# Hybrid decoder step: memory projections moved into the recurrent layer and a LayerNorm, recurrent blocks interleaved, weight splits in quarter pieces, high parts written in a row

## Chip, cores and metric

One core of a Trainium2 chip runs the whole step as one program. The metric is the device time of one execution in microseconds (us); lower is better. Engines: PE is TensorE, PEld its weight load, DVE is VectorE, ACT is ScalarE, POOL is GpSimd, SP only issues DMAs. Each has its own queue and waits only on semaphores.

## The reference, cut to what matters

Two layers are computed for 512 prompt tokens and 8 x 4 sample tokens (544 columns), with 1024 features. Layer 0 mixes with a gated linear recurrence (RG-LRU), layer 1 with a gated delta rule over 8 heads. Each then attends to 256 memory tokens and ends in a SwiGLU, dense in layer 0, top 2 of 8 experts in layer 1. Each of the six sub-layers ends in a LayerNorm.

```python
mem_k_p = einsum('bmd,lde->lbme', mem_prompt, xa_wk)      # memory projections, both layers
mem_v_p = einsum('bmd,lde->lbme', mem_prompt, xa_wv)
# recurrent mixer, layer 0
gate_branch, rec = split(x @ w_in)
rec, conv_new = causal_conv(rec, conv0, conv_w, conv_b)
gates = einsum('btnc,ncg->btng', blocks(rec), gate_w) + gate_b
r, i = sigmoid(gates[..., :BW]), sigmoid(gates[..., BW:])
log_a = -8.0 * r * softplus(-lam);  a = exp(log_a)
bterm = sqrt(-expm1(2.0 * log_a)) * i * rec
h[t] = a[t] * h[t-1] + bterm[t]
y = (h * gelu(gate_branch)) @ w_out
# each sub-layer
x = layer_norm(alpha * x + sublayer(x))
```

## The kernel before, in words

Activations stand with features on partitions: x is 8 tiles of 128 x 544. Products that must be close to fp32 are made of three passes in fp32r: an activation is split into a high part (xh, hh) and a low part (xl, hl), a weight tile into wh and wl. One weight tile of 128 outputs is a *slot*: SP loads it into one of four raw buffers, POOL makes wh and wl (`split`, two instructions of 1024 columns, two buffers each), and PE runs 48 matmuls on it in `lin_steps`: wh with xh, wl with xh, wh with xl. A *direct* slot is not split; PE reads raw in full fp32. The memory projections (16 slots a layer, `kv`) are direct. Slots are numbered in the order in which PE uses them, and the semaphores w_in, w_split and w_used count them, so SP, POOL, PE and the engine that evicts all follow one order that is written out by hand. DVE and ACT run their instructions strictly one after the other (`Serial`).

The order on PE: for each of four blocks of the recurrent layer two "rec" tiles, two "gelu" tiles and four gate groups; the output linear of 8 tiles (S_LOUT); LayerNorm 0 with the 16 projections of layer 0; attention 0; LayerNorm 1; the dense FFN (72 slots, PE lines 501 and 674); LayerNorm 2; the 32 matmuls for beta and decay ("wba", L724) and a chain on 8 partitions; 8 heads of the delta rule, where each head's projections of the next head fill PE's gaps; the output linear; LayerNorm 3 with the projections of layer 1; attention 1; LayerNorm 4 with the router; the experts on direct slots.

In a recurrent block ACT copies the rec tiles out, DVE convolves them (lines 1548 to 1558), PE multiplies by the gate weights (L706), which ACT loads at the start of the block into one buffer, ACT applies the sigmoids (L1146), exp, tanh and a square root, and DVE forms the recurrence in a scan. The root's argument 1 - a*a is made from tanh with a reciprocal (L1603). The two tiles of a block go through this one after the other.

A LayerNorm sums on PE (L523), subtracts the mean on DVE (L1433), squares on ACT (L1026), sums squares on PE (L530), multiplies on DVE (L1436), and then ACT writes for each k the high part xh (L1036) and the tile of x (L1038); DVE takes the low part xl (L1422). The next linear's first tile waits for ln_xh tile by tile in its first pass and for ln_xl in its third. In LayerNorms 0 and 3 three projections follow the sum on PE and 13 follow the squares (KV_EARLY = 3), and ACT evicts them between its own instructions.

## Time and profile before

| what | value |
|---|---|
| median of 3 runs | 2915.51 us (2908.92 to 2920.08) |
| profiled execution: time, span | 2916.7 us, 2914.5 us |
| granted TensorE clock, mean | 0.891 of full |
| PE busy | 2439.2 us, 84% of the span |
| DVE, ACT, POOL busy | 961.7, 580.2, 790.2 us |
| chain that ended last, by engine | PE 70%, DVE 16%, ACT 5%, DMA 4% |

The span is cut below by stages, as seen in the timeline: recurrent layer up to 269 us, its output linear to 320, LayerNorm 0 with projections to 388, attention 0 to 549, LayerNorm 1 to 582, dense FFN to 1024, LayerNorm 2 to 1065, beta stage to 1110, heads to 1840, output linear to 1891, LayerNorm 3 with projections to 1959, attention 1 to 2120, LayerNorm 4 and routing to 2200, experts to the end. The granted clock of PE is 1.00 at 2.4 GHz and 0.5 at 1.2 GHz; a value between is a mean over the stretch.

### The profile page before, as it was taken

The numbers are of one execution on the slowest core, as the hardware profiler recorded it, in microseconds if no ns is written. First come the engines' busy times: TensorE is split into PE (matmuls) and PEld (weight loads), VectorE is DVE, ScalarE is ACT, GpSimd is POOL, SyncE is SP. The second block draws the span as 40 slices with busy tenths as digits, with TensorE's granted clock in tenths as the row PEclk, the third lists the DMA queues.
The fourth block names the chain that finished last, engine by engine and source line by source line (L and its number), as shares of the span: only waits on it lengthen the run. The fifth ranks groups of instructions, "written<-read, shape, count | busy, mean of one in ns | idle before, by whom it ended". The sixth has DMA issues, their size and how long they took to land.

```text
span 2914.5 us, 42825 instructions
## 1 busy us (share of the span) xinstructions
PE 2439.2 (84%) x17284; PEld 2293.5 (79%) x17284; DVE 961.7 (33%) x1473; ACT 580.2 (20%) x1086; POOL 790.2 (27%) x389
## 2 busy tenths in 40 slices
PE   6664998899999945888777886899959999999994
PEld 5654895799999925887767875897748999999994
DVE  6774302411011046565556564321240100000003
ACT  2232312211001032322233222032130000000113
POOL 4421250477677602221111220314310000000001
PEclk9876999899999976887777886899969999999996
DMA  5112444122222201111111110354125667777885
GB/s 196 51 43 74 149 141 159 58 80 86 81 86 87 86 15 46 46 47 45 40 44 45 45 46 16 106 195 170 59 91 188 207 193 240 248 250 263 281 279 169
DMA packets 97656, 346.06 MB, mean 119 GB/s; under 512 B 13440, under 2 KB 18688, under 8 KB 92528
## 3 DMA queue, kind: packets, MB, share of 16 engines
q1 hardware_dynamic: 73136, 279.08, 29.6%
q10 hardware_dynamic: 18368, 43.60, 4.3%
q0 software_dynamic: 6016, 21.43, 2.1%
q8 instruction: 101, 1.65, 0.2%
q14 instruction: 35, 0.29, 0.0%
HBM read 317.61 MB, written 26.47 MB: 118 GB/s over the span
## 4 chain that ended last, share of the span: by engine, by line
PE 70%; DVE 16%; ACT 5%; DMA 4%; issue 2%; POOL 0%; DVEq 0%; ACTq 0%; SPq 0%; POOLq 0%
PE ps L501 25%; PE ps L951 13%; PE ps L966 7%; PE ps L674 5%; DVE work L1551 2%; DMA raw<-weights 2%; PE ps L552 2%; PE ps L548 2%; PE ps L530 2%; PE ps L797 2%; PE ps L706 1%; PE ps L809 1%; DVE work L1553 1%; PE ps L806 1%; PE ps L781 1%
## 5 line engine op out<-in xcount | busy, mean ns | idle before, releaser
L426 POOL TENSOR_TENSOR wh<-raw,tab 128x1024 fp32r<-128x1024 f32 x168 | 323.7, 1927 | 1343.3 <-PE ps L501 1150.6
L951 PE MATMUL ps<-work,raw 128*128 128x128 f32 (+6 forms) x3072 | 423.8, 299 | 15.7 <-DMA raw<-weights 12.4
L428 POOL TENSOR_TENSOR wl<-raw,wh 128x1024 fp32r<-128x1024 f32 x168 | 430.7, 2564 | 13.2
L951 PEld LDWEIGHTS ps<-work,raw 128*128 128x128 f32 x3072 | 419.3, 191 | 18.9 <-issue 6.9
L501 PE MATMUL ps<-xh,wh 128*128 128x272 f32 x2048 | 310.5, 304 | 71.4 <-ACT work L1126 28.7
L501 PEld LDWEIGHTS ps<-xh,wh 128*128 128x128 f32 x2048 | 284.0, 200 | 78.2 <-issue 41.4
L501 PE MATMUL ps<-xh,wl 128*128 128x272 f32 x2048 | 289.2, 291 | 0.0
L501 PE MATMUL ps<-xl,wh 128*128 128x272 f32 x2048 | 285.7, 289 | 0.0
L501 PEld LDWEIGHTS ps<-xh,wl 128*128 128x128 f32 x2048 | 270.2, 191 | 0.3
L501 PEld LDWEIGHTS ps<-xl,wh 128*128 128x128 f32 x2048 | 265.9, 188 | 0.0
L966 PE MATMUL ps<-work,raw 128*128 128x128 f32 (+6 forms) x1536 | 217.9, 298 | 1.1 <-DVE work L1878 0.8
L966 PEld LDWEIGHTS ps<-work,raw 128*128 128x128 f32 x1536 | 209.6, 190 | 1.9 <-DVE work L1878 1.4
L470 POOL DMA_DIRECT2D rows_y<-moe_h x8 | 4.3, 538 | 658.6 <-DVE moe_h L1871 658.6
L1878 DVE TENSOR_TENSOR work<-moe_h,ps 128x128 f32<-128x128 f32 (+6 forms) x96 | 30.7, 319 | 441.3 <-ACT moe_h L1354 441.3
L1354 ACT ACTIVATE moe_h<-ps 128x128 f32<-128x128 f32 (+6 forms) x96 | 29.1, 303 | 399.1 <-PE ps L951 399.0
L1500 DVE TENSOR_TENSOR work<-work,ps 128x544 f32<-128x544 f32 x24 | 17.3, 722 | 232.0 <-PE ps L501 232.0
L1551 DVE SCALAR_TENSOR_TENSOR work<-work 128x568 f32<-128x568 f32 x64 | 90.0, 1407 | 2.3
L1871 DVE COPY moe_h<-ps 128x256 f32<-128x256 f32 (+1 forms) x64 | 25.1, 392 | 197.6 <-PE ps L939 155.7
L674 PE MATMUL ps<-hh,wh 128*128 128x272 f32 x384 | 80.8, 292 | 5.9 <-DVE hl L1422 5.9
L674 PE MATMUL ps<-hh,wl 128*128 128x272 f32 x384 | 79.9, 291 | 0.0
L674 PE MATMUL ps<-hl,wh 128*128 128x272 f32 x384 | 79.9, 290 | 0.0
L706 PE MATMUL ps<-work 128*128 128x272 f32 x128 | 41.1, 491 | 38.5 <-DMA work<-lru_gate 33.8
...
## 6 DMA issues: line engine op xcount, KB each, us to landing
raw<-weights SPq DMA_DIRECT2D x488, 512.0 KB, 3.8
...
moe_h<-rows_x POOLq DMA_DIRECT2D x14, 512.0 KB, 8.0
rows_x<-lnsq ACTq DMA_DIRECT2D x9, 512.0 KB, 7.1
...
```

Source lines behind the costliest of these rows:

```text
L426: nc.gpsimd.tensor_tensor(flat(h1), flat(r1), one_col, MUL).then_inc(pool_hi, 1)
L428: nc.gpsimd.tensor_tensor(flat(l1), flat(r1), flat(h1).bitcast(F), SUB).then_inc(w_split, 1)
L501: last = mm(ps[:, 2 * i + h, 0:HT], w[:, par_, k, :], a[:, k, h * HT:(h + 1) * HT], start=(n == 0 and k == 0), stop=(n == 2 and k == KT - 1))
L530: last = mm(ps[:, 6 + h, 0:HT], ones, lnsq[:, k % 2, h * HT:(h + 1) * HT], start=(k == 0), stop=(k == KT - 1))
L548: last = mm(ps[:, b, 0:MEM], raw[:, q, k, :], A_mem[:, k, :], start=(k == 0), stop=(k == KT - 1))
L552: last = mm(ps[:, b, mt * P:(mt + 1) * P], A_mem[:, k, mt * P:(mt + 1) * P], raw[:, q, k, :], start=(k == 0), stop=(k == KT - 1))
L674: last = mm(ps[:, 2 * d + h, 0:HT], w[:, s % 2, k, :], a[:, f, h * HT:(h + 1) * HT], start=(f == 0 and m == 0), stop=(f == FT - 1 and m == 2))
L706: last = mm(ps[:, 4 + 2 * (g % 2) + h, 0:HT], L_gw[:, 4 * k + g, :], L_rec[:, k, h * HT:(h + 1) * HT], start=(k == 0), stop=(k == 1))
L797: last = mm(ps[:, 4, c * P:(c + 1) * P], G_bl[:, v % 2, c, :], G_t[:, c, :], start=True, stop=True)
L951: last = mm(ps[:, j // 2, (j % 2) * c:(j % 2 + 1) * c], raw[:, slot % RAW, k, :], M_x[:, r % 2, k, 0:c], start=(k == 0), stop=(k == KT - 1))
L966: last = mm(ps[:, 2 + d % 2, 0:c], raw[:, slot % RAW, k, :], M_h[:, f, 0:c], start=(f == 0), stop=(f == FT - 1))
L1551: s(V.scalar_tensor_tensor(acc, ext[:, j:j + CONV], w(j), acc, MUL, ADD))
```

## The change

- **Projections of layer 0.** They leave LayerNorm 0 and go into the recurrent layer: four before the first rec tiles, four after the first gelu tiles, four after the second, four after the last gates. Memory, its first weights and x are loaded in another order at the start. Keys and values get room that the recurrent layer leaves free.
- **Projections of layer 1.** They leave LayerNorm 3: seven go into LayerNorm 2, nine behind the wba matmuls. ACT evicts the nine between the steps of the beta chain.
- **Recurrent layer.** PE runs block b+1's rec tiles ahead of block b's gates. DVE convolves block b+1 ahead of block b's recurrence. Buffers are doubled, the gate weights of block b+1 are loaded after block b's sigmoids, loops are unrolled, and the root's argument is (1 + a*a) * tanh, without a reciprocal.
- **wba.** The two groups of 8 outputs go to partitions 0 and 32 of the same banks, and each k waits for its own tile of x.
- **Splits.** POOL makes each high and each low part in four instructions of 256 columns (PIECES = 4).
- **LayerNorm.** ACT writes the eight high parts in a row, then the eight tiles of x.

The core of the diff; most removed lines and repeated parts are left out:

```diff
-KV_EARLY = 3
+KV_EARLY, KV_MID = 3, 7
...
-RAW, SPLIT = 4, 2
+RAW, SPLIT, PIECES = 4, 2, 4
...
+        S_KV0 = [0, 8, 16, 28]
+        S_LRU = [4, 12, 20, 24]
+        S_LOUT = 32
+        S_Q = [S_LOUT + 8, None]
         S_O = [S_Q[0] + 8, None]
         S_FFN = S_O[0] + 8
...
+        S_KV1 = S_FFN + HALVES * 36
+        S_GDN = S_KV1 + 16
...
+        A_v = moe_h[:, S0:S0 + MT * D].rearrange("p (a b) -> p a b", b=D)
+        A_k = moe_h[:, S1:S1 + KT * MEM].rearrange("p (a b) -> p a b", b=MEM)
...
+            load(0, None, W_KV0, 0, 2)
+            sp.dma_start(x[:, :, :], I["xT"]).then_inc(ld_x, 16)
+            load(0, None, W_KV0, 2, 4)
+            turns(S_LRU[0], RAW, None, None, W_LRU)
+            turns(S_KV0[1], RAW, 4, None, W_KV0 + 4)
+            turns(S_LRU[1], RAW, None, None, W_LRU + 4)
+            turns(S_KV0[2], RAW, 8, None, W_KV0 + 8)
+            turns(S_LRU[2], RAW, None, None, W_LRU + 8)
+            turns(S_LRU[3], RAW, 12, None, W_LRU + 12)
+            turns(S_KV0[3], RAW, 12, None, W_KV0 + 12)
+            turns(S_LOUT, 8, None, 16, W_LOUT)
             for l in range(NL):
...
+                d = 16 * (l + 1)
+                turns(S_Q[l], 8, d, d, W_Q0 if l == 0 else W_Q1)
+                turns(S_O[l], RAW, d, d, (W_Q0 if l == 0 else W_Q1) + 8)
+                cache(l)
+                turns(S_O[l] + RAW, RAW, d, d, (W_Q0 if l == 0 else W_Q1) + 8 + RAW)
                 if l == 0:
...
+                    turns(S_FFN, HALVES * 36, 16, 16, W_FFN)
+                    turns(S_KV1, 16, 16, None, W_KV1)
+                    turns(S_GDN, 4 * GH + 8, None, 32, W_GDN)
...
-                    nc.gpsimd.tensor_tensor(flat(h1), flat(r1), one_col, MUL).then_inc(pool_hi, 1)
-                    pool.wait_ge(pool_hi, t * RAW + (j + 1 - offset))
-                    nc.gpsimd.tensor_tensor(flat(l1), flat(r1), flat(h1).bitcast(F), SUB).then_inc(w_split, 1)
+                    for q in range(PIECES):
+                        k0, k1 = q * KT // PIECES, (q + 1) * KT // PIECES
+                        nc.gpsimd.tensor_tensor(flat(h1[:, k0:k1]), flat(r1[:, k0:k1]), one_col, MUL).then_inc(pool_hi, 1)
+                    for q in range(PIECES):
+                        k0, k1 = q * KT // PIECES, (q + 1) * KT // PIECES
+                        pool.wait_ge(pool_hi, PIECES * t * RAW + (PIECES * (j - offset) + q + 1))
+                        low = nc.gpsimd.tensor_tensor(flat(l1[:, k0:k1]), flat(r1[:, k0:k1]), flat(h1[:, k0:k1]).bitcast(F), SUB)
+                    low.then_inc(w_split, 1)
...
                 if l is not None:
-                    kv(l, KV_EARLY, 16)
+                    kv(l, KV_EARLY, KV_MID)
...
+                    if l == 0 and 4 <= t < 12 and t % 4 < 2:
+                        pe.wait_ge(lru_gelu, 2 * (t // 4) - 2 + t % 4 + 1)
+                    elif l == 0 and t >= 12 and t % 4 < 2:
+                        pe.wait_ge(lru_gelu, 6 + t % 4 + 1)
+                    elif t >= 2:
+                        pe.wait_ge(kv_ev, 16 * l + t - 1)
...
+            def lru_rec(b):
                 for j in range(2):
...
+                    if b in (1, 2, 0):
+                        pe.wait_ge(kv_ev, 4 * b + 3 + j)
+                    else:
+                        pe.wait_ge(lru_gelu, 2 * (b - 1) + j + 1)
+                    lin_tile(S_LRU[b] + j, 4 * (min(b, 2) + 1), j, j, xh, xl, fresh=0 if b == 0 and j == 0 else None,
...
+            def lru_gel(b):
                 for j in range(2):
...
+                    pe.wait_ge(lru_ext, 2 * b + j + 1)
+                    lin_tile(S_LRU[b] + 2 + j, 4 * (min(b, 2) + 1), j, j, xh, xl)
+            def lru_gates(b):
+                pe.wait_ge(lru_gw_in, 16 * (b + 1))
+                pe.wait_ge(lru_conv, 2 * b + 2)
                 for g in range(4):
...
+                    ge(pe, lru_gate_ev, 4 * b + g - 1)
                     for k in range(2):
                         for h in range(2):
                             last = mm(ps[:, 4 + 2 * (g % 2) + h, 0:HT], L_gw[:, 4 * k + g, :],
...
+                                      L_rec[:, b % 2, k, h * HT:(h + 1) * HT], start=(k == 0), stop=(k == 1))
                     last.then_inc(lru_gate_full, 1)
...
+            kv(0, 0, 4)
+            lru_rec(0)
+            lru_gel(0)
+            kv(0, 4, 8)
+            lru_rec(1)
+            lru_gates(0)
+            lru_gel(1)
+            kv(0, 8, 12)
+            lru_rec(2)
+            lru_gates(1)
+            lru_gel(2)
+            lru_rec(3)
+            lru_gates(2)
+            lru_gel(3)
+            lru_gates(3)
+            kv(0, 12, 16)
+            pe.wait_ge(kv_ev, 16)
             pe.wait_ge(lru_y, 8)
...
-            layer_norm(0, 0)
+            linear(S_LOUT, 16, hh, hl, z_ready, 0)
...
-            layer_norm(2)
-            pe.wait_ge(ln_xl, KT * 3)
-            for g in range(2):
...
-                        last = mm(ps[0:GH, 4 + 2 * g + h, 0:HT], pc("wba", 16 * k + 8 * g, 16 * k + 8 * g + 8),
+            layer_norm(2, 1)
+            for k in range(KT):
+                pe.wait_ge(ln_x, KT * 2 + k + 1)
+                for h in range(2):
+                    for g in range(2):
+                        last = mm(ps[32 * g:32 * g + GH, 4 + h, 0:HT], pc("wba", 16 * k + 8 * g, 16 * k + 8 * g + 8),
                                   x[:, k, h * HT:(h + 1) * HT], start=(k == 0), stop=(k == KT - 1))
             last.then_inc(b_pe, 1)
+            kv(1, KV_MID, 16)
+            pe.wait_ge(kv_ev, 32)
...
+            act.dma_start(A_mem, I["memT"].rearrange("p (a b) -> p a b", b=MEM)).then_inc(mem_in, 16)
             act.dma_start(tab[:, :], I["tables"]).then_inc(ld_tab, 16)
...
+            kv(0, 0)
+            kv(0, 1)
             act.wait_ge(ld_x, 16)
             for k in range(KT):
                 s(A(xh[:, k, :], x[:, k, :], ACT.Copy), x_split_h, k + 1)
+            kv(0, 2)
+            kv(0, 3)
...
+                if n < NLN - 1:
+                    for k in range(KT):
+                        act.wait_ge(ln_n, n * KT + k + 1)
+                        s(A(xh[:, k, :], x[:, k, :], ACT.Identity, bias=pc("lnb", n * 8 + k, n * 8 + k + 1),
+                            scale=pc("lng", n * 8 + k, n * 8 + k + 1)), ln_xh, n * KT + k + 1)
                 for k in range(KT):
                     act.wait_ge(ln_n, n * KT + k + 1)
-                    if n < NLN - 1:
...
                     s(A(x[:, k, :], x[:, k, :], ACT.Identity, bias=pc("lnb", n * 8 + k, n * 8 + k + 1),
                         scale=pc("lng", n * 8 + k, n * 8 + k + 1)), ln_x, n * KT + k + 1)
...
+                    if l is not None and k < KV_MID - KV_EARLY:
...
+            def sigmoid(b):
+                ge(act, lru_dve, 6 * (b - 1) + 6)
                 for g in range(4):
...
+                    act.wait_ge(lru_gate_full, 4 * b + g + 1)
                     dst = (L_r, L_i)[g // 2]
...
+                    s(A(two(dst[:, g % 2, :]), pair(2 + g % 2), ACT.Sigmoid, bias=lgb[:, 2 * b + g % 2, g // 2:g // 2 + 1]),
+                      lru_gate_ev, 4 * b + g + 1)
+                if b + 1 < BLK:
+                    gate_weights(b + 1)
+            def decays(b):
                 for j in range(2):
...
+                    act.wait_ge(lru_dve, 6 * b + j + 1)
+                    s(A(L_a[:, j, :], L_r[:, j, :], ACT.Exp, scale=-1.0))
+                    s(A(L_t[:, j, :], L_r[:, j, :], ACT.Tanh), lru_act, 4 * b + j + 1)
+            def root(b, j):
+                act.wait_ge(lru_dve, 6 * b + j + 3)
+                s(A(L_t[:, j, :], L_t[:, j, :], ACT.Sqrt), lru_act, 4 * b + j + 3)
+            def high_part(b, j):
+                act.wait_ge(lru_dve, 6 * b + j + 5)
+                s(A(hh[:, 2 * b + j, :], L_b[:, j, :], ACT.Copy), lru_yh, 2 * b + j + 1)
+            ext(0)
+            gelu(0)
+            for t in range(4, 8):
+                kv(0, t)
+            for b in range(BLK - 1):
+                ext(b + 1)
+                sigmoid(b)
+                decays(b)
+                root(b, 0)
+                root(b, 1)
+                gelu(b + 1)
+                high_part(b, 0)
+                high_part(b, 1)
+                if b == 0:
+                    for t in range(8, 12):
+                        kv(0, t)
+            b = BLK - 1
+            sigmoid(b)
+            decays(b)
+            kv(0, 12)
+            root(b, 0)
+            root(b, 1)
+            kv(0, 13)
+            high_part(b, 0)
+            kv(0, 14)
+            high_part(b, 1)
+            kv(0, 15)
+            kv_out(0)
             act.wait_ge(lru_y, 8)
...
-            layer_norm(0, 0)
+            piece(0, 0)
+            act.wait_ge(w_used, S_LOUT + 8)
+            piece(0, 1)
+            piece(0, 2)
...
+            act.wait_ge(w_used, S_KV1)
+            act.dma_start(A_mem, I["memT"].rearrange("p (a b) -> p a b", b=MEM)).then_inc(mem_in, 16)
+            layer_norm(2, 1)
             act.wait_ge(b_pe, 1)
             s(A(two(B_r[1])[0:GH], pair(2)[0:GH], ACT.Sigmoid), b_act, BETA)
+            kv(1, KV_MID)
             act.wait_ge(b_dve, ARGUMENT)
             s(A(B_r[5][0:GH, :], B_r[5][0:GH, :], ACT.Exp, scale=-1.0))
             s(A(B_r[9][0:GH, 0:1], pc("alog")[0:GH, :], ACT.Exp), b_act, RATE)
+            for t in range(KV_MID + 1, 13):
+                kv(1, t)
             act.wait_ge(b_dve, SUMS)
             s(A(B_r[2][0:GH, :], B_r[0][0:GH, :], ACT.Exp))
             s(A(B_r[3][0:GH, :], B_r[3][0:GH, :], ACT.Exp), b_act, GROWN)
+            for t in range(13, 16):
+                kv(1, t)
+            kv_out(1)
             act.wait_ge(b_dve, ROWED)
...
-            kv_start(1)
-            layer_norm(3, 1)
+            act.wait_ge(w_used, S_GOUT + 8)
+            for i in range(RING):
+                piece(1, i)
+            layer_norm(3)
...
-                    s(V.tensor_scalar(L_b, L_t, 1.0, None, ADD))
-                    s(V.reciprocal(L_b, L_b))
-                    s(V.scalar_tensor_tensor(L_t, L_t, 2.0, L_b, MUL, MUL), lru_dve, b * 10 + (3 * j + 5))
...
+                    dve.wait_ge(lru_act, 4 * b + j + 1)
+                    s(V.tensor_tensor(L_b[:, j, :], L_a[:, j, :], L_a[:, j, :], MUL))
+                    s(V.scalar_tensor_tensor(L_t[:, j, :], L_b[:, j, :], 1.0, L_t[:, j, :], ADD, MUL), lru_dve, 6 * b + j + 3)
+                for j in range(2):
+                    k = 2 * b + j
...
+                    dve.wait_ge(lru_act, 4 * b + j + 3)
+                    s(V.tensor_tensor(bt, t, L_i[:, j, :], MUL))
...
+                    s(V.tensor_tensor_scan(t, a, bt, 0.0, MUL, ADD))
...
+                    dve.wait_ge(lru_gelu, 2 * b + j + 1)
+                    s(V.tensor_tensor(bt, t, L_gel[:, 2 * (b % 2) + j, :], MUL), lru_dve, 6 * b + j + 5)
+                for j in range(2):
+                    k = 2 * b + j
+                    dve.wait_ge(lru_yh, 2 * b + j + 1)
+                    split_low(hl[:, k, :], L_b[:, j, :], hh[:, k, :], lru_y, 2 * b + j + 1)
+            lru_convolve(0)
+            for b in range(BLK):
+                if b + 1 < BLK:
+                    lru_convolve(b + 1)
+                lru(b)
```

## Rows read from the trace of the kernel before

**Rows 1.** Windows: stretch, length, busy PE PEld DVE ACT POOL, clock, DMA share, GB/s.

```profile
0.00:10.00 10.00, 0.00 (x0) 0.00 (x0) 0.00 (x0) 1.28 (x1) 1.15 (x5) 1.00 0.81 310
24.00:269.00 245.00, 146.72 (x897) 135.98 (x897) 165.26 (x224) 76.31 (x105) 75.41 (x32) 0.78 0.18 58
582.00:1024.00 442.00, 434.58 (x3442) 433.75 (x3440) 47.20 (x65) 33.75 (x51) 314.22 (x143) 0.99 0.27 84
1110.00:1840.00 730.00, 579.89 (x3824) 531.87 (x3824) 423.93 (x655) 201.21 (x387) 145.19 (x64) 0.79 0.14 42
```

**Rows 2.** Groups by line, 95 to 270 us: busy, mean ns, idle before.

```profile
L1603 DVE RECIPROCAL work<-work 128x544 f32<-128x544 f32 x7 | 24.9, 3553 | 0.2
```

**Rows 3.** The chain that ended last, whole span: start, us, what.

```profile
0.76 9.48 DMA x<-xT
...
107.06 4.19 DMA work<-lru_gate
...
227.81 10.34 PE ps L706 x32
...
341.10 17.27 PE ps L548 x80
358.37 28.60 PE ps L552 x256
```

**Rows 4.** Timeline around LayerNorms 0 and 1: start, us, engine, line, operation.

```profile
317.42 2.16 PE L501 MATMUL ps<-hl,wh 128*128 128x272 f32 x16
...
391.60 2.16 PE L501 MATMUL ps<-xl,wh 128*128 128x272 f32 x16
...
546.74 1.91 PE L501 MATMUL ps<-xl,wh 128*128 128x272 f32 x14
...
578.86 0.84 ACT L1036 ACTIVATE xh<-x,par 128x544 fp32r<-128x544 f32 x1
...
585.38 2.16 PE L501 MATMUL ps<-xl,wh 128*128 128x272 f32 x16
```

**Rows 5.** Timeline, router in LayerNorm 4.

```profile
2150.78 5.39 PE L900 MATMUL ps<-par,x 128*128 128x8 f32 x40
```

**Rows 6.** Timeline: sample scores, then the beta stage, on PE.

```profile
441.94 1.91 PE L568 MATMUL ps<-moe_h 128*32 128x256 f32 x32
...
1065.02 17.07 PE L724 MATMUL ps<-x,par 128*8 128x272 f32 x64 [17.25 <-DVE xl L1422]
...
1107.24 1.98 PE L731 MATMUL ps<-tab,work 8*128 8x8 f32 x20 [25.14 <-DVE work L1659]
```

**Rows 7.** The page's DMA issues: count, KB, us to landing.

```profile
raw<-weights SPq DMA_DIRECT2D x488, 512.0 KB, 3.8
```

**Rows 8.** Timeline: POOL at start and in the FFN, small DVE.

```profile
0.26 0.10 POOL L2028 MEMSET const-float32-0.0<- 128x1 f32 x1 [0.26 <-issue]
...
0.75 0.95 POOL L415 MEMSET lnsq<- 128x1024 f32 x1 [0.29 <-POOLq L2028]
...
28.16 0.17 DVE L1519 TENSOR_TENSOR work<-work 128x8 f32<-128x8 f32 x1
...
623.62 1.89 POOL L426 TENSOR_TENSOR wh<-raw,tab 128x1024 fp32r<-128x1024 f32 x1 [1.16 <-PE ps L501]
625.59 2.39 POOL L428 TENSOR_TENSOR wl<-raw,wh 128x1024 fp32r<-128x1024 f32 x1
...
631.65 2.77 POOL L428 TENSOR_TENSOR wl<-raw,wh 128x1024 fp32r<-128x1024 f32 x1
```

**Rows 9.** Timeline, recurrent layer, POOL and DVE.

```profile
161.02 2.34 POOL L428 TENSOR_TENSOR wl<-raw,wh 128x1024 fp32r<-128x1024 f32 x1
161.09 2.85 DVE L1621 TENSOR_TENSOR work<-work 128x544 f32<-128x544 f32 x1
```

**Rows 10.** The chain in one head.

```profile
1465.23 2.75 DVE work L1553
...
1482.22 0.76 DVE work L1553
```

283 lines of the change are left out of this document (106 added, 177 removed).

## The prediction

> **What bounds the kernel now.** I read the stage windows first, then the chain that ended last, then the timeline of each stage the diff touches. PE is the bound on average, but it is full only in some stages: 434.6 of 442 us in the dense FFN, against 146.7 of 245 us in the recurrent layer and 579.9 of 730 us in the gated-delta heads [rows 1]. In the recurrent layer the chain alternates between PE gates, a 3.55 us reciprocal per tile on DVE, and a gate-weight load of 4.2 to 4.5 us before each of blocks 1 to 3 [rows 2, 3]. Nothing is queued on PE for those times. The 16 memory-projection tiles of a layer are the opposite case: they sit in LayerNorms 0 and 3, and their 13 later tiles run as one unbroken PE block on the chain, 17.3 us for five key tiles and 28.6 us for eight value tiles [rows 3]. So there is idle PE in one place and 56 us of movable PE work in another.
>
> The profiled execution took 2916.7 us around a span of 2914.5; the median of the three runs is 2915.5, so I sum against 2916.7 and take 1 us off.
>
> **LayerNorms 0 and 3.** From the end of the linear before to the end of the first tile after, LayerNorm 0 takes from 319.6 to 393.6, 74.0 us. LayerNorm 1, which has no projections, takes from 548.7 to 587.4, 38.7 us, its cold PE included [rows 4]. The projections leave, so 35.3 us leave, twice. LayerNorm 3's window has the same length. The cache pieces that ACT loads keep their conditions and are needed over 80 us later.
>
> **High parts in a row.** ACT needs 0.84 us and a gap of 0.03 for each of the 16 writes [rows 4]. Before, the eighth high part came 14 us after the first write began, and two more passes of 16 matmuls followed. Now it comes after 7 us, the middle pass follows at once, and the last pass is paced by x tiles that still end at 14 us: last x, 0.8 us for its low part, two matmuls. The first tile ends near 583.6 in place of 587.4 in LayerNorm 1's times, so -3.8 us for each of LayerNorms 0, 1 and 3. LayerNorm 4 goes the other way. Its consumer reads x, not the high parts, so it starts 6 us later; 40 router matmuls take 10.8 us there (two groups, one of 5.4 us [rows 5]) plus 2.8 us of transposes. That ends near 2160.3 in place of 2156.2: +4. Sum of these parts with the 35.3 twice: -70.6 - 11.4 + 4 = -78.
>
> **LayerNorm 2 and the beta stage.** Seven projections go into LayerNorm 2, nine behind the 32 wba matmuls. By LayerNorm 0's old pacing, the seven delay the last x tile by about 11 us, to 1074.6. But the wba matmuls now go k by k behind ln_x and no longer wait for all the low parts. Their two groups write column groups 0 and 1. 16 score matmuls of 32 columns, in four column groups, took 1.9 us (32 records), 0.12 us each, against 0.43 for a full-width one of the same 256 columns (17.3 us for 40) [rows 3, 6]: different column groups run together. So wba costs about 7.5 us in place of 17.1, mostly under ln_x, and ends near 1076.5 in place of 1082.1. Nine projections of 3.5 us then end at 1108.6, and kv_ev 32 holds the 8-row transposes to 1109.2; they stood at 1107.2 behind the DVE chain [rows 6], which this change starts 5.6 us earlier and so hides. The first head tile then starts 2 us later, warm, and saves about 2. I take 0, bounds -3 and +8. If wba did not pair up it would be +8.
>
> **Recurrent layer.** Start: x now queues behind two weight tiles, while ACT's queue brings the memory, tables and gates. About 5.9 MB must pass before x is complete, at the 310 to 350 GB/s of the start [rows 1]; x lands near 17.5 us and not at 10.2 [rows 3]. Four projections fill PE meanwhile; splitting x again takes its time, and the first tile starts as if at 27.5 (24.2 before).
> PE's list from there to the last gelu tile: 16 tiles of 6.0 us (a tile's period, from the starts at 625.59 and 631.65 [rows 8]), 8 projections of 3.5 us, 3 gate groups. A gate group took 10.3 us because PE was at half clock in its first part. Kept busy, 16 matmuls of 272 columns cost 16 x 0.43 x 272/256 = 7.3 us. 27.5 + 96 + 28 + 22 = 173.5.
> DVE decides the end. It had 165 us in 245, 41 per block. Each block loses two reciprocals and adds (8.0 us), gains two multiplies (1.5) and drops the parameter copies (some 1): 34 per block, lock waits included. The third block's recent part starts about 156 (end of rec 3), conv 3 and lru 2 end near 181, and sigmoid 3 waits for that, so two gates stand until 181 and end at 185.5. The last block's own tail was 30.7 us, from the gates' end at 238.2 [rows 3] to 268.9. Two reciprocals with their adds go (8.0), one exp and one sqrt table load (2.6), and the two halves overlap on ACT and DVE: 18. Projections 12 to 15, 14.3 us, lie inside that. 185.5 + 18 = 203.5, and I add 5 for splits that DVE's work stretches, see below: 209. That is -60, bounds -40 and -75. Each recurrent tile's 0.5 MB load waits on SP behind a projection's release: 3.8 us to land [rows 7] and 4.4 to split, 8.2 of the 10.5 us that three more projections take, so hidden with 2 us to spare; the projections' evictions (0.38 us each on ACT) and the two output DMAs have ACT's idle time. The gate-weight loads are issued a block ahead, at no cost while three PE groups stand between; without that cover 4.5 each.
>
> **Split in eight pieces.** This touches every split slot. A POOL instruction and a DVE one with two SBUF inputs exclude each other: a 0.73 us multiply that began at 161.09 took 2.85, to just past the end of the POOL piece at 163.36, then its own time [rows 9]. With quarter pieces a single DVE wait is at most a quarter as long, but POOL comes back four times as often. For a lone DVE instruction that is a gain; for a burst that outlasts the split, the total blocked time is POOL's own, before and after. Heads have both kinds: L1553 took 2.75 beside a split and 0.76 without [rows 10]; four such waits per head, 6.8 us, lie on the chain, and two of the three places are bursts. I take 0 for the heads, bounds -40 and +20.
> The price is the fixed cost of six more instructions. A slot has 6.06 us; POOL uses 1.89 + 0.08 + 2.39, or 2.77 where DVE interferes, so 1.7 or 1.3 us are free: 0.22 to 0.28 us per added instruction [rows 8]. No row shows a quarter piece. From below: a one-column memset took 0.10. From above: if multiply moved data as fast as the 1024-column memset (0.95), the fixed part were 1.0 us. The nearest in kind is DVE's TENSOR_TENSOR of 8 columns, 0.17 us; it fits under the limit, so 0 [rows 8]. The added POOL time in the heads, 1 us a split, is inside their bounds.
>
> The Trainium skill ("SBUF — State Buffer", section "SBUF: two separate sides") says that the shared port pair is an exclusive lock held for the whole instruction, which the two durations above bear out. Taken alone it favours short pieces, the third rival below. Its page "GPSIMD Engine Reference", section "Performance versus the Vector engine", gives 4497 ns for a two-input fp32 operation of 2048 columns; with 2.39 for our 1024 that is an estimate of 0.28 us fixed, at the limit, which speaks against this edit and belongs to the first rival.
>
> **Sum.** -78 + 0 - 60 + 0 = -138. 2916.7 - 138 - 1 = 2778.
>
> **Rivals.**
> *POOL becomes the bound of the full stages.* 72 FFN and 48 linear tiles have the 6.06 us period. At 0.30 us fixed the slot is short by 0.1 or 0.5, at 0.4 by 0.7 or 1.1: 36 to 108 us over 120 tiles, 2815 to 2885. For it: the free time is under a third of the slot, and nothing measures a piece. Against: the 0.10 us of the small memset and the 0.17 of DVE. Chance 0.18.
> *The recurrence stays chain-bound.* Serial waits of ACT and DVE, and splits stretched to 8 us while DVE is busy, keep the output linear at 235. 2804. For: DVE was busy 67% and its lock waits are in that. Chance 0.14.
> *Short pieces free DVE.* Of the 6.8 us per head, 5 go, 8 times: 2738. Chance 0.14.
> *Slower.* One mechanism: an added POOL instruction costs over 0.42 us. From there the shortage, 6 x 0.42 - 1.5 = 1.05 us, times 120 plus some 12 for the heads, eats the whole 138; at 0.5 it is 180 + 15, so 2778 + 195 = 2973. The bound of 1.0 from above allows it. Chance 0.07.
> The forecast itself has 0.47, range 2755 to 2803.
>
> **Numbers.** The range reaches from the freed DVE to most of the POOL case: 2735 to 2865. A difference under 0.5% (15 us) can't be told from none. Faster: all but the slow case and the thin edge before it, 0.91; same 0.02; slower 0.07.
>
> **What would show it.** Output linear of the recurrent layer starting near 209, gate groups near 7.3 us, no gate-weight wait on the chain; 35 us between the linears around LayerNorms 0 and 3; no projection in either; quarter POOL pieces under 0.65 us (high) and 0.8 (low), POOL idle at each FFN slot and PE's FFN still near 442; wba near 8 us. Wrong if PE waits for POOL in the FFN, if PE idles before gate groups, or if the heads' 88 us period moves by over 3 us.

## The result and the profile after

The changed kernel takes 2772.0 us (median of 4 runs, 2767.2 to 2775.8) against 2915.2 for the kernel before on the same chip, a ratio of 0.951 (0.9485 to 0.9534). The forecast was 2778. That the sum came this close is partly luck: gains of 20.9 us that it had missed and losses of 17.9 us that it had missed nearly cancel (last point of the account below). Milestones read from PE's timeline, in us of the two profiled executions (spans 2914.5 and 2773.5):

| stretch | before | after | change | predicted |
|---|---|---|---|---|
| start to output linear of the recurrent layer | 268.9 | 213.3 | -55.6 | -60 |
| LayerNorm 0, to the end of the next first tile | 74.0 | 32.9 | -41.1 | -39.1 |
| LayerNorm 1, same | 38.7 | 32.2 | -6.6 | -3.8 |
| dense FFN | 436.4 | 437.4 | +1.0 | 0 |
| LayerNorm 2 and beta, to the first head tile | 86.1 | 90.3 | +4.2 | 0 |
| heads, to their output linear | 731.2 | 717.6 | -13.6 | 0 |
| LayerNorm 3, as 0 | 73.7 | 32.2 | -41.6 | -39.1 |
| LayerNorm 4, to the experts' first transposes | 70.8 | 79.1 | +8.3 | +4 |
| linears, attentions, experts | | | +4.0 | 0 |
| sum | | | -141.0 | -138 |

The window of the recurrent layer of the kernel after, up to the last gelu tile (columns as in [rows 1]):

```profile
28.00:182.00 154.00, 149.52 (x1058) 142.51 (x1059) 96.76 (x162) 55.29 (x88) 91.12 (x120) 0.99 0.39 129
```

PE is busy 149.5 of 154 us, where it had 146.7 of 245 in the whole layer before [rows 1], at a granted clock of 0.99. Its own timeline, with the idle time ahead of a row and its releaser in brackets:

```profile
27.86 3.77 PE L534 MATMUL ps<-xh,wh 128*128 128x272 f32 x16 [2.23 <-issue]
...
129.91 3.95 PE L748 MATMUL ps<-work 128*128 128x272 f32 x16 [0.33 <-ACT work L1210]
...
147.67 2.24 PE L534 MATMUL ps<-xh,wh 128*128 128x272 f32 x16 [1.81 <-POOL wl L458]
...
155.63 2.24 PE L534 MATMUL ps<-xh,wh 128*128 128x272 f32 x16 [1.72 <-POOL wl L458]
...
187.43 5.63 PE L748 MATMUL ps<-work 128*128 128x272 f32 x16 [1.91 <-ACT work L1210]
192.89 14.45 PE L589 MATMUL ps<-raw,work 128*128 128x128 f32 x128
213.32 1.93 PE L534 MATMUL ps<-hh,wh 128*128 128x272 f32 x7 [5.97 <-DVE hl L1528]
```

The gate-weight loads are gone from PE's waits. Two new waits are for POOL; its timeline there shows why. A split in quarters takes about 5.2 us where DVE does not interfere (5.16 in the FFN, shown below). Beside DVE's recurrence four low pieces take 4.26 us and the four high pieces behind them 3.79, together more than the 6 us of a tile:

```profile
143.26 4.26 POOL L458 TENSOR_TENSOR wl<-raw,wh 128x256 fp32r<-128x256 f32 x4
147.49 3.79 POOL L454 TENSOR_TENSOR wh<-raw,tab 128x256 fp32r<-128x256 f32 x4
151.24 4.24 POOL L458 TENSOR_TENSOR wl<-raw,wh 128x256 fp32r<-128x256 f32 x4
```

The router in LayerNorm 4 before, PE's timeline (its second group is [rows 5]), and the window of both groups (PE, PEld, DVE, ACT, POOL, clock, DMA, GB/s):

```profile
2140.38 1.26 PE L900 MATMUL ps<-par,x 128*128 128x8 f32 x10 [4.19 <-ACT x L1038]
2142.13 6.11 PE L900 MATMUL ps<-par,x 128*128 128x8 f32 x30 [0.48 <-ACT x L1038]
...
2140.30:2156.30 16.00, 15.31 (x92) 14.80 (x92) 9.22 (x14) 13.59 (x18) 0.00 (x0) 0.64 0.00 1
```

The beta stage and the router after, and the window of the router. The router's first group starts behind 10.30 us of idle time in place of 4.19. Its second group of 40 takes 7.96 us in place of 5.39, at a granted clock of 0.50 in the whole window in place of 0.64. The wba group takes 7.51 us in place of 17.1 [rows 6] and waits for nothing. What waits in LayerNorm 2 are the projections ahead of it, 3.81 us, for an eviction (L1080) that stands on ACT behind the eight high parts:

```profile
961.24 9.84 PE L585 MATMUL ps<-work,raw 128*128 128x256 f32 x32 [3.81 <-ACT moe_h L1080]
971.01 7.51 PE L782 MATMUL ps<-x,par 128*8 128x272 f32 x64
...
1995.72 8.12 PE L960 MATMUL ps<-par,x 128*128 128x8 f32 x40 [10.30 <-ACT x L1120]
...
2006.39 7.96 PE L960 MATMUL ps<-par,x 128*128 128x8 f32 x40
...
1995.70:2014.40 18.70, 18.63 (x92) 18.17 (x92) 5.80 (x8) 7.67 (x10) 0.00 (x0) 0.50 0.00 1
```

The chain of waits of the kernel after has something new at the start of the heads: a store of the rows of beta, which go through DRAM. In the kernel before, this store is not among DVE's waits there. Now 2 MB of keys and values are issued on ACT's queue right ahead of it:

```profile
1013.67 9.96 DMA scratch<-work
...
1024.54 4.67 DMA work<-gdn_hist
```

### The profile page after: what moved, and what is told of

Read it like the earlier page. It is cut to its first block, busy times and chain, and to the rows that moved or that the text cites. A ratio compares the mean times of both kernels' runs of the same rounds, so it can differ in the third digit from the quotient of the medians.

```text
span 2773.5 us, 43947 instructions
## 1 busy us (share of the span) xinstructions
PE 2434.3 (88%) x17284; PEld 2290.4 (83%) x17284; DVE 868.2 (31%) x1445; ACT 569.5 (21%) x1078; POOL 980.2 (35%) x1397
## 4 chain that ended last, share of the span: by engine, by line
PE 75%; DVE 10%; ACT 6%; DMA 5%; issue 2%; POOL 1%; ACTq 0%; DVEq 0%; SPq 0%; POOLq 0%
PE ps L534 29%; PE ps L1011 13%; PE ps L1026 8%; PE ps L710 5%; DMA raw<-weights 3%; PE ps L563 2%; PE ps L857 2%; PE ps L585 2%; PE ps L869 2%; PE ps L589 2%; PE ps L866 1%; PE ps L841 1%; PE ps L921 1%; DVE x L1542 1%; PE ps L623 1%
## 5 line engine op out<-in xcount | busy, mean ns | idle before, releaser
L454 POOL TENSOR_TENSOR wh<-raw,tab 128x256 fp32r<-128x256 f32 x672 | 433.7, 676 | 1016.3 <-PE ps L534 816.4
L458 POOL TENSOR_TENSOR wl<-raw,wh 128x256 fp32r<-128x256 f32 x672 | 517.8, 800 | 0.0
L1011 PEld LDWEIGHTS ps<-work,raw 128*128 128x128 f32 x3072 | 419.6, 191 | 20.9 <-issue 13.7
L534 PE MATMUL ps<-xh,wh 128*128 128x272 f32 x2048 | 316.1, 306 | 24.9 <-ACT xh L1116 11.1
L534 PEld LDWEIGHTS ps<-xh,wh 128*128 128x128 f32 x2048 | 284.1, 200 | 36.7 <-issue 26.1
L585 PE MATMUL ps<-work,raw 128*128 128x256 f32 x256 | 61.9, 405 | 13.2 <-DMA work<-memT 7.1
L1559 DVE SCALAR_TENSOR_TENSOR x<-x,ps 128x544 f32<-128x544 f32 x32 | 23.1, 721 | 157.8 <-PE ps L534 157.8
```

Of the source, the lines that this page charges most:

```text
L454: nc.gpsimd.tensor_tensor(flat(h1[:, k0:k1]), flat(r1[:, k0:k1]), one_col, MUL).then_inc(pool_hi, 1)
L458: low = nc.gpsimd.tensor_tensor(flat(l1[:, k0:k1]), flat(r1[:, k0:k1]), flat(h1[:, k0:k1]).bitcast(F), SUB)
L534: last = mm(ps[:, 2 * i + h, 0:HT], w[:, par_, k, :], a[:, k, h * HT:(h + 1) * HT], start=(n == 0 and k == 0), stop=(n == 2 and k == KT - 1))
L585: last = mm(ps[:, b, 0:MEM], raw[:, q, k, :], A_mem[:, k, :], start=(k == 0), stop=(k == KT - 1))
L1011: last = mm(ps[:, j // 2, (j % 2) * c:(j % 2 + 1) * c], raw[:, slot % RAW, k, :], M_x[:, r % 2, k, 0:c], start=(k == 0), stop=(k == KT - 1))
```

## The experiments

A ratio is the kernel's time over that of the kernel before, both measured on the same chip; between experiments, ratios are compared. The changed kernel itself has 0.951. Milestones come from one profiled execution of each kernel.

### Pieces: whole splits in the changed kernel

```diff
-RAW, SPLIT, PIECES = 4, 2, 4
+RAW, SPLIT, PIECES = 4, 2, 1
```

> The changed kernel with each split in two whole instructions again. My theory after reading the trace of the changed kernel: the short pieces, priced at 0 in the prediction, gave most of the 2.6 us per head and part of the 6.4 us of LayerNorm 1. Then the heads' period goes from 85.3 back to about 88 us, LayerNorm 1 from 32.3 to about 34.5, the dense FFN from 437.3 to about 436, and the time from 2772 to about 2797. Rival: the heads and the LayerNorms are shorter because PE's clock is granted higher (0.906 against 0.891) since the projections went; then whole splits change the heads by under 0.5 us each and the time stays within 5 us of 2772. Second rival: the 8 us by which the last gelu tile comes late are the price of the pieces (PE waited for POOL twice); then the recurrent layer's output linear starts near 205 in place of 213.

Measured: 2797.9 us, ratio 0.9599 (0.9569 to 0.9629). Heads 734.1 us in place of 717.6, their period (from one head's first tile to the next head's) up to 87.9 in place of 85.3; LayerNorms 0 and 3 both 34.0 in place of 32.9 and 32.2, LayerNorm 1 32.7, FFN 435.1, output linear at 215.5. PE's clock is 0.904 here too, so the clock's rival falls, and so does the one that put the late gelu tile down to the pieces (it ends at 181.0). The first theory holds for the heads; in LayerNorm 1 the pieces gave 0.5 us, not 2.

What the pieces do in a head is seen in the same burst of DVE in both kernels. With whole splits, the timeline of DVE and POOL:

```profile
1207.46 1.89 POOL L454 TENSOR_TENSOR wh<-raw,tab 128x1024 fp32r<-128x1024 f32 x1 [9.45 <-PE ps L534]
1207.95 4.82 DVE L1656 SCALAR_TENSOR_TENSOR work<-work 128x568 f32<-128x568 f32 x2
1209.43 2.73 POOL L458 TENSOR_TENSOR wl<-raw,wh 128x1024 fp32r<-128x1024 f32 x1
1212.81 0.75 DVE L1658 SCALAR_TENSOR_TENSOR work<-work 128x512 f32<-128x512 f32 x1
1213.59 0.25 DVE L1662 SCALAR_TENSOR_TENSOR work<-work 128x28 f32<-128x28 f32 x1
1213.87 0.22 DVE L1663 SCALAR_TENSOR_TENSOR work<-work 128x4 f32<-128x4 f32 x1
```

With quarter pieces, the kernel after:

```profile
1203.04 3.87 POOL L454 TENSOR_TENSOR wh<-raw,tab 128x256 fp32r<-128x256 f32 x4 [7.63 <-PE ps L534]
1203.53 1.89 DVE L1656 SCALAR_TENSOR_TENSOR work<-work 128x568 f32<-128x568 f32 x2
1205.45 0.98 DVE L1658 SCALAR_TENSOR_TENSOR work<-work 128x512 f32<-128x512 f32 x1
1206.47 0.48 DVE L1662 SCALAR_TENSOR_TENSOR work<-work 128x28 f32<-128x28 f32 x1
1206.87 3.75 POOL L458 TENSOR_TENSOR wl<-raw,wh 128x256 fp32r<-128x256 f32 x4
1206.98 0.62 DVE L1663 SCALAR_TENSOR_TENSOR work<-work 128x4 f32<-128x4 f32 x1
```

In this burst the two engines take turns. With whole splits two DVE instructions pay for the split's 4.6 us, and the burst of five takes 6.1 us. With quarters each DVE instruction waits for one piece, even the small ones (0.48 and 0.62 us for 0.25 and 0.22), the burst takes 4.1, and it is POOL that is late: 7.6 us for the split. POOL is not among PE's nine largest waits in the heads; DVE heads that list, with 35.7, 35.3 and 24.0 us. Over all heads DVE's busy time, which includes its waits for POOL, falls from 422.4 to 396.4 us, and POOL's rises from 144.9 to 205.9. Two groups of DVE's lines over all heads, whole and then quarters:

```profile
L1656 DVE SCALAR_TENSOR_TENSOR work<-work 128x568 f32<-128x568 f32 x48 | 71.0, 1479 | 1.7
L1829 DVE TENSOR_TENSOR work<-work,tab 128x512 f32<-128x512 f32 x56 | 60.1, 1073 | 1.9
```

```profile
L1656 DVE SCALAR_TENSOR_TENSOR work<-work 128x568 f32<-128x568 f32 x48 | 46.6, 971 | 1.7
L1829 DVE TENSOR_TENSOR work<-work,tab 128x512 f32<-128x512 f32 x56 | 43.1, 770 | 1.9
```

### Pieces alone in the kernel before

```diff
-RAW, SPLIT = 4, 2
+RAW, SPLIT, PIECES = 4, 2, 4
...
-                    nc.gpsimd.tensor_tensor(flat(h1), flat(r1), one_col, MUL).then_inc(pool_hi, 1)
+                    for q in range(PIECES):
...
+                        nc.gpsimd.tensor_tensor(flat(h1[:, k0:k1]), flat(r1[:, k0:k1]), one_col, MUL).then_inc(pool_hi, 1)
...
```

> The kernel before with nothing but the splits in quarter pieces. If the pieces free DVE at short waits and cost PE nothing: heads' period 88 to about 85.5, LayerNorms 1, 2 and 4 some 2 us shorter each, dense FFN 436 to 437.5, recurrent layer within 3 us of 269; time about 2915 - 27 = 2888. If the heads' gain comes from elsewhere: within 5 us of 2915. If the pieces cost where PE is full, over 2920.

Measured: 2880.6 us, ratio 0.9869 (0.9843 to 0.9896). Heads 713.8 us in place of 731.2, FFN 439.3, LayerNorms 1, 2 and 4 at 37.8, 84.7 and 71.5. The heads came as expected, the LayerNorms hardly moved, and what I had not expected is the recurrent layer: its output linear starts at 245.6 in place of 268.9. There DVE's busy time falls from 165.3 to 148.7 us and PE's waits for ACT's copies (L1126) from 28.7 to 12.7 us. That DVE's waits lay on that layer's chain in the kernel before fits both, but no run separates them. In the changed kernel the same pieces are worth 2.2 us.

### Output transfers behind the rows

```diff
-            kv_out(1)
             act.wait_ge(b_dve, ROWED)
...
             rows(0)
+            kv_out(1)
```

> The changed kernel with the two output transfers of layer 1's keys and values (2 MB) issued behind the rows of the first head and not ahead of the scratch store. Theory: they held the scratch store up for 8 us, which the first head's convolution waited for, and that is why the heads gained 13.6 us and not 21. Then the store lands about 2 us after its issue, the output linear of the gated-delta layer starts 7 to 9 us earlier against the first head tile, and the time is 2772 - 8 = 2764. Rival: the first head has slack, since PE has other tiles; then the store is early and the time stays at 2772 within 3 us.

Measured: 2774.6 us, ratio 0.9504 (0.9474 to 0.9533): no difference. DVE's wait for the scratch store falls from 10.6 to 3.4 us, but its wait for ACT behind the convolution grows from 6.1 to 10.0. From the first head tile to the second head's first tile it is 54.7 us in place of 56.4, so at most 1.7 us of the 8 counted. Even these are not sure: with the reciprocal put back (below) and the transfers left where they were, that stretch is 54.8 us too. The chain between them, in this kernel, runs through the splits of the next tiles:

```profile
1019.93 2.33 POOL wh L454 x4
1022.26 3.62 POOL wl L458 x4
```

The theory was wrong in size: the wait was real and mostly covered. (The heads' stretch was 713.6 here, but 2.9 of those 4 us come in the last head, whose end is 147.7 or 150.6 us from one run to the next, with either place of the transfers.)

### Order of ACT's writes, tile by tile

```diff
-                if n < NLN - 1:
-                    for k in range(KT):
-                        act.wait_ge(ln_n, n * KT + k + 1)
-                        s(A(xh[:, k, :], ...), ln_xh, n * KT + k + 1)
                 for k in range(KT):
                     act.wait_ge(ln_n, n * KT + k + 1)
+                    if n < NLN - 1:
+                        s(A(xh[:, k, :], ...), ln_xh, n * KT + k + 1)
                     s(A(x[:, k, :], ...), ln_x, n * KT + k + 1)
```

> The changed kernel with ACT writing high part and tile of x in turn for each k, as before. The prediction priced the row order at -3.8 us for each of LayerNorms 0, 1 and 3 and +4 for LayerNorm 4. By that: LayerNorms 0 and 3 from 33.0 and 32.2 to about 36.5, LayerNorm 1 from 32.3 to 36, LayerNorm 4's stretch to the first transposes from 79.1 to 75; the time goes up by about 7 us to 2779. By what the trace of after shows (+8.2 in LayerNorm 4) the sum is only +3: 2775. Rival: the order is worth nothing because DVE's low parts pace the third pass either way; then LayerNorm 1 stays within 1 us.

Measured: 2778.4 us, ratio 0.951 (0.948 to 0.954). LayerNorms 0, 1 and 3: 37.8, 37.0 and 36.7 us, so the row order is worth 4.9, 4.8 and 4.5. LayerNorm 4: 71.8 in place of 79.1, so it costs 7.3 there. LayerNorm 2 with beta: 85.7 in place of 90.3, a cost of 4.6 that I had not priced at all. Net 14.2 - 11.9, some 2 us, which the two times can't tell apart. In LayerNorm 4 the router starts 7.1 us sooner than in the changed kernel, at the same clock (0.50). In LayerNorm 2 it is not wba that gains: the last four of the seven projections take 13.9 us without a wait in place of 20.7 with the wait for the eviction, and wba now waits 0.8 us for tiles of x.

### The reciprocal put back

```diff
-                    s(V.tensor_tensor(L_b[:, j, :], L_a[:, j, :], L_a[:, j, :], MUL))
-                    s(V.scalar_tensor_tensor(L_t[:, j, :], L_b[:, j, :], 1.0, L_t[:, j, :], ADD, MUL), ...)
+                    s(V.tensor_scalar(L_b[:, j, :], L_t[:, j, :], 1.0, None, ADD))
+                    s(V.reciprocal(L_b[:, j, :], L_b[:, j, :]))
+                    s(V.scalar_tensor_tensor(L_t[:, j, :], L_t[:, j, :], 2.0, L_b[:, j, :], MUL, MUL), ...)
```

> The changed kernel with the root's argument made from tanh with an add and a reciprocal again, as in the kernel before (one DVE instruction more per tile, the reciprocal among them). Theory: PE bounds the recurrent layer up to the last gelu tile (it is busy 149.5 of the 154 us from 28 to 182), so DVE's extra time is hidden in the first three blocks and counts in the last block's tail alone: 2 x (3.6 + 0.7 - 1.0) = about 6.5 us. Then the last gelu tile ends at 182 as now, and the output linear starts at 213 + 6.5 = 220; time 2772 + 6 = 2778. Rival: DVE's chain paces every block; then all four blocks lose 6.5 us and the linear starts at 239, the time is 2798.

Measured: 2799.5 us, ratio 0.9602 (0.9586 to 0.9618); last gelu tile at 191.8, last gates at 210.8, output linear at 236.5. My theory fell: 23 us, near the rival's 26. Some 10 us are lost up to the last gelu tile and 13 behind it. PE's waits in this layer, in the kernel with the reciprocal (total, times, longest):

```profile
PE ps L748 <- ACT work L1210: 9.3, 4, 8.3
PE ps L534 <- ACT work L1203: 5.2, 1, 5.2
...
PE ps L589 <- ACT work L1203: 4.3, 1, 4.3
```

L1203 is the gelu. It stands on ACT behind the roots, and a root waits for DVE's argument, as ACT's timeline of block 0 shows:

```profile
96.58 1.28 ACT L1223 ACT_TABLE_LOAD   x1 [3.59 <-DVE work L1694]
...
101.42 0.66 ACT L1223 ACTIVATE work<-work 128x544 f32<-128x544 f32 x1 [2.89 <-DVE work L1694]
102.09 1.28 ACT L1203 ACT_TABLE_LOAD   x1
```

Without the reciprocal the gelu's table load starts at 95.8 and its second tile waits for PE instead. So a busy PE (149.5 of 154) did not mean slack on DVE: the two were level, through ACT's queue.

### No filler between the recurrent blocks

Loads, splits and evictions follow the new numbers, and x is loaded first.

```diff
-        S_KV0 = [0, 8, 16, 28]
-        S_LRU = [4, 12, 20, 24]
+        S_KV0 = [16, 20, 24, 28]
+        S_LRU = [0, 4, 8, 12]
...
-            kv(0, 12, 16)
+            kv(0, 0, 16)
```

> The changed kernel with all 16 projections of layer 0 behind the last gates; the rest of the recurrent layer as it is. Theory: PE's list sets the pace, so without its 8 middle projections (27.8 us) and with x loaded first the last gelu tile ends some 30 us earlier, near 150, and the gates near 163; of the 56 us of projections some 20 lie under the last block's tail and the linear starts near 163 + 57 = 220, 7 us later than now: only about half of the filler is free. Rival: the recurrence's own chain of ACT and DVE sets the pace and the fillers are all free; then the last gates still end near 190 and the linear starts near 247, and the time is 2772 + 34 = 2806.

Measured: 2784.2 us, ratio 0.955 (0.9534 to 0.9566); last gelu tile ends at 153.4, last gates at 164.6, output linear starts at 221.4. As expected of PE's list. Moving 12 projections, 42 us of PE work, into the blocks and the start saves 8 us over leaving them all at the end. What the new order of the blocks gives by itself, without the shorter argument and the pieces, was not run.

### x first, and mixed order

Both have the output transfers behind the rows. In the one, LayerNorms 2 and 4 write the tiles of x first and then each high part as a copy of its tile; in the other they write tile by tile. LayerNorms 0, 1 and 3 keep the row order.

```diff
-                if n < NLN - 1:
+                if n in (0, 1, 3):
...
+                if n in (2, 4):
+                    for k in range(KT):
+                        s(A(xh[:, k, :], x[:, k, :], ACT.Copy), ln_xh, n * KT + k + 1)
```

> The changed kernel with the output transfers of keys and values behind the first head's rows, and in LayerNorms 2 and 4, where PE's next work reads x, the eight tiles of x ahead of the eight high parts (each then a copy of its tile). With tile by tile in every LayerNorm the two stretches took 85.7 and 71.8 us in place of 90.3 and 79.1; here the last tile of x comes 7 us earlier still. Theory: LayerNorm 2 with beta about 82 us, LayerNorm 4 to the first transposes about 68, heads 714: 2772 - 8 - 11 - 4 = 2749. Rival: DVE's chains behind the low parts, which now come last, eat it; then 86 and 76, about 2762.

Measured: 2758.5 us, ratio 0.9465 (0.9449 to 0.9481); LayerNorm 2 with beta 83.5, LayerNorm 4 72.7, heads 717.5.

> As the kernel with x first, but LayerNorms 2 and 4 write tile by tile as the kernel before, LayerNorms 0, 1 and 3 keep the high parts in a row. By the run with tile by tile everywhere: LayerNorms 0, 1, 3 at 33, 32, 32 us, LayerNorm 2 with beta 85.7, LayerNorm 4 71.8, heads 714: 2772 - 4.6 - 7.3 - 4 = 2756. If the order's price in LayerNorm 4 was the clock and not the order, LayerNorm 4 stays near 79 and the time is 2763.

Measured: 2758.8 us, ratio 0.946 (0.9444 to 0.9476); LayerNorm 2 with beta 85.7, LayerNorm 4 70.9, heads 717.3. Both beat the changed kernel by about 13 us. In LayerNorm 4 x first brings nothing more, as PE's timeline of that kernel shows:

```profile
1979.68 8.12 PE L960 MATMUL ps<-par,x 128*128 128x8 f32 x40 [3.32 <-ACT x L1120]
...
1990.36 7.96 PE L960 MATMUL ps<-par,x 128*128 128x8 f32 x40
```

and the mixed order's:

```profile
1986.45 1.22 PE L960 MATMUL ps<-par,x 128*128 128x8 f32 x10 [4.19 <-ACT x L1123]
1988.20 6.11 PE L960 MATMUL ps<-par,x 128*128 128x8 f32 x30 [0.53 <-ACT x L1123]
...
1996.86 5.38 PE L960 MATMUL ps<-par,x 128*128 128x8 f32 x40
```

PE waits 3.3 us in place of 4.2: tile by tile it was not starved for long anyway (0.53 us). And with x first the router's matmuls ran at a granted clock of 0.50 (1979.6 to 1998.4) in place of 0.64 (1986.4 to 2002.3), so that the second group took 7.96 us and not 5.38. That is more than the 1.8 us by which x first is behind, so the order by itself gained a little there and the clock took it back.

### Halves and eighths

```diff
-RAW, SPLIT, PIECES = 4, 2, 4
+RAW, SPLIT, PIECES = 4, 2, 2
```

and the same with 8, both on the mixed-order kernel.

> The mixed-order kernel with splits in four pieces, halves, in place of eight quarters. A whole instruction (1.9 to 2.4 us) gave a heads' period of 87.9 us, a quarter 85.3. If DVE's wait goes with the length of the piece, halves give half of what separates them from none: the period would be 85.3 + (87.9 - 85.3) x (1/2 - 1/4)/(1 - 1/4) = 86.2, the heads 723 in place of 717.3, the time 2759 + 6 = 2765; the dense FFN 0.5 to 1 us shorter. Rival: a DVE burst needs one gap only, so halves do all: period 85.3, time 2757. Second rival: only quarters help, since a half is still longer than the DVE instructions: 87.9, time 2775.

Measured: 2764.2 us, ratio 0.9485 (0.9466 to 0.9503); period 86.2 to 87.7, heads 724.2, FFN 437.9. As expected: between whole splits and quarters, what the heads lose goes with the length of the piece.

> The mixed-order kernel with splits in sixteen pieces of 128 columns. Uncontended, a split took 2.33 + 2.82 = about 5.1 us in quarters against 4.36 whole: 0.13 us for each added instruction. Eight more make 6.2 us, over PE's 6.0 us a tile: POOL becomes the bound in the dense FFN and the linears, 0.2 to 0.5 us a tile. Expected: dense FFN from 438 to 452 to 475 us, each linear of 8 tiles 2 to 4 us longer, the heads no better than 717; time 2759 + 25 to 60, about 2800. Rival: the fixed cost shrinks with the piece and POOL stays under the slot: 2757.

Measured: 2833.8 us, ratio 0.9719 (0.9698 to 0.974); FFN 475.3, attentions 163 and 162 in place of 156, LayerNorms 0 and 3 39.0, heads 714.2 in place of 717.3. The FFN came at the end of my range and the time above it, since I had left out the attentions and LayerNorms. The heads were even a little shorter than the 717 that I had set as their best. Tiles of the FFN start at 605.54, 611.76 and 618.47 here, 6.2 and 6.7 us apart. The splits without DVE beside them, from POOL's timeline in the FFN, whole (kernel before, at 599.62), halves, quarters and eighths, one fence for each of the last three:

```profile
498.51 2.04 POOL L454 TENSOR_TENSOR wh<-raw,tab 128x512 fp32r<-128x512 f32 x2 [0.98 <-PE ps L534]
500.51 2.53 POOL L458 TENSOR_TENSOR wl<-raw,wh 128x512 fp32r<-128x512 f32 x2
```

```profile
497.75 2.33 POOL L454 TENSOR_TENSOR wh<-raw,tab 128x256 fp32r<-128x256 f32 x4 [0.41 <-PE ps L534]
500.03 2.83 POOL L458 TENSOR_TENSOR wl<-raw,wh 128x256 fp32r<-128x256 f32 x4
```

```profile
527.89 2.91 POOL L454 TENSOR_TENSOR wh<-raw,tab 128x128 fp32r<-128x128 f32 x8
530.76 3.39 POOL L458 TENSOR_TENSOR wl<-raw,wh 128x128 fp32r<-128x128 f32 x8
```

1.89 + 2.39 = 4.28 us in 2 instructions, 4.57 in 4, 5.16 in 8, 6.30 in 16: 0.14 to 0.15 us for each one added. Quarters leave 0.9 us of a 6.05 us slot, eighths nothing.

The added fixed cost is not all. The FFN multiplies on DVE that read two tiles from SBUF, 24 in 430 us, in groups by line (20 of them), quarters and then eighths, and one of the latter in DVE's timeline:

```profile
L1528 DVE TENSOR_TENSOR hl<-work,hh 128x544 f32 x20 | 22.0, 1099 | 21.4 <-ACT hh L1179 21.4
...
L1531 DVE TENSOR_TENSOR hl<-work,hh 128x544 f32 x20 | 104.7, 5235 | 21.4 <-ACT hh L1182 21.4
...
581.15 5.28 DVE L1531 TENSOR_TENSOR hl<-work,hh 128x544 f32 x1 [1.06 <-ACT hh L1182]
```

With quarters such a multiply took 1.1 us. With eighths it took 5.2: the one shown began beside a POOL piece and ended at 586.4, while POOL ran twelve more or less back to back to 585.86 and then paused for 0.18 us. So here DVE did not get its turn behind one piece, as it does in the burst of a head, but only where POOL paused. Why the two cases differ is open. PE's wait for these multiplies in the FFN is 14.8 us in place of 6.7.

### The parts together

On the mixed-order kernel, with x first in LayerNorm 2 alone, whole splits in the FFN alone, and the third group of projections one place later:

```diff
-            kv(0, 8, 12)
             lru_rec(2)
             lru_gates(1)
             lru_gel(2)
+            kv(0, 8, 12)
             lru_rec(3)
...
-            turns(S_LOUT, S_KV1 - S_LOUT, 4, 16)
+            turns(S_LOUT, S_FFN - S_LOUT, 4, 16)
+            turns(S_FFN, S_KV1 - S_FFN, 0, 16, 1, (PIECES - 1) * (S_FFN - 16))
```

> The best parts together: mixed order with x first in LayerNorm 2 alone, output transfers behind the rows, whole splits in the dense FFN and quarters elsewhere, and the third group of layer 0's projections between the third gelu tiles and the fourth rec tiles, so that POOL has time to make the fourth block's splits (PE waited 3.5 us for them). Against the mixed-order kernel: LayerNorm 2 with beta 83.6 in place of 85.7, FFN 435.1 in place of 438.8, output linear of the recurrent layer at 210 in place of 213.6; sum -9: 2750. Rival for the moved group: the wait for POOL is DVE's lock on the splits and comes back elsewhere; then the linear stays at 213.

Measured: 2756.1 us, ratio 0.9462 (0.9443 to 0.948), no better than the mixed order. LayerNorm 2 with beta is 83.4 as expected. The output linear starts at 211.8, and PE still waits twice for POOL, 3.5 us, now in the third block's tiles: in both layouts POOL falls behind where eight split tiles follow each other beside the recurrence, which is the rival's case. The FFN took 437.5, not 435.1; its stretch lay between 435.1 and 439.3 in every run but the eighths, and the pieces' price in it can't be told from that spread.

### The argument without the reciprocal, alone

```diff
-                    s(V.tensor_scalar(L_b, L_t, 1.0, None, ADD))
-                    s(V.reciprocal(L_b, L_b))
-                    s(V.scalar_tensor_tensor(L_t, L_t, 2.0, L_b, MUL, MUL), ...)
+                    s(V.tensor_tensor(L_b, L_a, L_a, MUL))
+                    s(V.scalar_tensor_tensor(L_t, L_b, 1.0, L_t, ADD, MUL), ...)
```

> The kernel before with nothing but the root's argument as a*a + 1 times tanh, without the reciprocal. It asks how much of the recurrent layer's 56 us that edit gives by itself. In the kernel before the chain alternates between DVE's steps, PE's gates and the load of the gate weights, so every block should lose its own DVE time, 2 x (3.6 + 0.7 - 1.0) = 6.5 us, four times: output linear at 269 - 26 = 243, time 2889. Rival: the gate-weight load (PE waited 33.8 us for it in three waits) or PE's own list paces the first three blocks; then only the tail gains 6.5 us: linear at 262, time 2909.

Measured: 2889.3 us, ratio 0.9919 (0.99 to 0.9938); output linear at 245.7. The chain theory holds: 23.2 of the 26 us. PE's wait for the gate weights is gone from the list, and 25.6 us of waits for the convolution stand in its place.

## Why the prediction was right, point by point

- **Projections out of LayerNorms 0 and 3.** Right: of 41.1 and 41.6 us the row order is 4.9 and 4.5 and the pieces 1.1 and 1.8 (by the run with whole splits), which leaves 35.1 and 35.3 against 35.3.
- **High parts in a row.** -3.8 three times was right in kind (4.5 to 4.9). LayerNorm 4's +4 was too small: the router does start 6 us later, as said, but the sum gave both its groups 5.4 us, as the second one took before; the first had taken 7.9 then, and after, at a granted clock of 0.50, they took 8.1 and 8.0. By the run tile by tile, at the same clock, the order costs 7.3. And the step failed for LayerNorm 2, which I left out of it: +4.6, since the evictions of the projections queue on ACT behind the row of high parts and PE waits 3.81 us for one of them.
- **LayerNorm 2 and beta.** The 0 for projections and wba was right: 85.7 us with the order undone, 86.1 before. wba took 7.51 us for a predicted 7.5. Not foreseen was the store behind the key and value transfers; it cost at most 1.7 us in the first head.
- **Recurrent layer.** -55.6 for -60. From the first tile to the end of the last gelu tile PE took 153.8 us, not 146: first tile 1.6 longer, the other 15 nearly 6.1 us each and not 6.0 (1.3), three gate groups 7.7 and not 7.3 (1.2, of which 0.96 are waits for ACT), the two tiles that waited for POOL 3.9, projections 0.2 less. From there it went nearly as drawn: 11.3 us to the gates' end (12), 20.3 to the linear (18). With the start 0.4 later that is 9.8 us over the drawn 203.5; the 5 us set aside for stretched splits cover half of it. "DVE decides the end" holds for the tail and, as the reciprocal put back shows, very nearly for the blocks: PE and the chain over DVE and ACT were level. The two single-edit runs show that the argument (-23.2) and the pieces (-23.3) each shortened the old chain by over 40% of what the layer gained; I had priced the first inside the new schedule and the second at nothing.
- **Splits.** 0 for the FFN was right: 0.14 to 0.15 us for an added instruction against 0.17 taken and a limit of 0.22 to 0.28. The estimate from the Trainium skill's page "GPSIMD Engine Reference" (section "Performance versus the Vector engine"), 0.28, was twice what the runs show. 0 for the heads was the wrong term: -16.5 us by the run with whole splits, partly eaten by the slower first head. The step that failed is "for a burst that outlasts the split, the total blocked time is POOL's own, before and after". Measured, DVE's busy time in the heads fell by 26.0 us, though POOL's own work grew. In the burst shown there are five DVE instructions, about 3 us of own work (2 x 0.8 + 0.75 + 0.25 + 0.22), against a split of 4.3 us in eight pieces. Taking turns piece by piece, the burst ends first and POOL carries the rest. That the other bursts go the same way is argued from the sum over all heads, not shown one by one. So the third rival was true, at 2 us a head and not 5.
- **Signs.** Of the signs of being wrong none came clearly: PE did not wait for POOL in the FFN, the period moved by 2.6 us and not over 3, and PE idled before gate groups 0.3 us three times and 1.9 once. One figure of the slow rival is off: 6 x 0.42 - 1.5 is 1.02 us, not 1.05, which changes nothing.
- **Where the sum closed.** Missed gains: 13.6 in the heads, 7.3 in LayerNorms 0, 1 and 3. Missed losses: 4.4 in the recurrent layer, 8.5 in LayerNorms 2 and 4, 5 in the FFN, linears, attentions and experts. 138 + 20.9 - 17.9 = 141.
